# A four-layer kernel for one core: small powers on GpSimd, scan kernels in four column strips, filler products ahead of the first input, and side work in shorter portions

## What is computed

```python
# layer 0 (cut): x is normed, multiplied by w_in, keys and values are compressed
y = _nsa_mixer(_rmsnorm(h, params[0]), *params[1:])
blk = k[:, cmp_idx] + pe[:, None, :]
return jax.nn.silu(blk @ w1) @ w2

# layer 1 (cut): the scan's step and its input factor
dt = jnp.exp(log_dt.astype(f32))[:, None]
mag = jnp.exp(lre * dt)
ab_re = mag * jnp.cos(lim * dt)
ab_im = mag * jnp.sin(lim * dt)
den = lre * lre + lim * lim
coef_re = (nr * lre + ab_im * lim) / den
coef_im = (ab_im * lre - nr * lim) / den
bb_re = coef_re[..., None] * br32 - coef_im[..., None] * bi32
```

## Time and profile before

| | us |
|---|---|
| median of 3 runs | 1860.41 |
| lowest, highest | 1859.4, 1860.86 |
| the profiled execution | 1856.59 |
| its span, first to last instruction | 1854.7 |
| TensorE busy in the span | 1784.1 (96%) |
| VectorE busy | 975.3 (53%) |
| ScalarE busy | 864.8 (47%) |
| GpSimd busy | 164.9 (9%) |
| chain that ended last: TensorE, VectorE, ScalarE | 82%, 10%, 5% |

### The profile page before, as it was taken

The page is one execution under the profiler, slowest core; times in us unless marked ns, Lnnn a source line. Parts: engine busy times, 40 slices in busy tenths (PEclk is TensorE's granted clock), DMA queues, the critical chain, the costliest instruction groups (busy, mean ns, idle before and its releaser), DMA issues.

```text
span 1854.7 us, 24520 instructions
## 1 busy us (share of the span) xinstructions
PE 1784.1 (96%) x9954; PEld 1455.8 (78%) x9954; DVE 975.3 (53%) x1680; ACT 864.8 (47%) x1486; POOL 164.9 (9%) x293
## 2 busy tenths in 40 slices
PE   5899998899999999999999999999999999999997
PEld 4677886679988877876877777888788878888886
DVE  7878556954764365345345545355544544434223
ACT  6355666645454244246345554266633643223223
POOL 2000226510000000000000000022200011111000
PEclk9899999999999999999999999999999999999999
DMA  3563441035423323311322223222132223322332
GB/s 132 159 213 122 132 115 58 1 100 212 151 95 102 103 80 115 101 57 48 111 90 80 69 70 101 94 69 63 55 108 94 92 69 100 102 94 88 105 94 65
DMA packets 61471, 181.30 MB, mean 98 GB/s; under 512 B 7136, under 2 KB 20256, under 8 KB 58928
## 3 DMA queue, kind: packets, MB, share of 16 engines
q1 hardware_dynamic: 61360, 179.75, 29.9%
HBM read 165.57 MB, written 16.25 MB: 98 GB/s over the span
## 4 chain that ended last, share of the span: by engine, by line
PE 82%; DVE 10%; ACT 5%; issue 1%; POOL 1%; DMA 0%; SPq 0%; DVEq 0%; ACTq 0%
PE bank L1002 19%; PE bank L1004 19%; PE bank L1003 18%; PE bank L1096 2%; PE bank L1097 2%; PE bank L1098 2%; PE bank L1259 2%; DVE wlo L2116 1%; PE bank L1238 1%; ACT L1525 1%; PE bank L1022 1%; PE bank L1023 1%; PE bank L1024 1%; PE bank L1228 1%; PE bank L1118 1%
## 5 line engine op out<-in xcount | busy, mean ns | idle before, releaser
L2116 DVE TENSOR_TENSOR wlo<-wraw,whi 128x1024 fp32r<-128x1024 f32 (+1 forms) x262 | 316.4, 1210 | 276.4 <-ACT whi L1520 275.2
L1002 PE MATMUL bank<-Hh,whi 128*128 128x512 f32 (+2 forms) x1104 | 442.9, 401 | 12.2 <-DVE wlo L2116 12.2
L1004 PE MATMUL bank<-Hh,wlo 128*128 128x512 f32 (+2 forms) x1104 | 432.4, 392 | 0.0
L1003 PE MATMUL bank<-Hl,whi 128*128 128x512 f32 (+2 forms) x1104 | 432.1, 391 | 0.0
L1520 ACT ACTIVATE whi<-wraw 128x1024 fp32r<-128x1024 f32 (+1 forms) x262 | 271.9, 1041 | 297.5 <-PE bank L1004 227.6
L1002 PEld LDWEIGHTS bank<-Hh,whi 128*128 128x128 f32 (+2 forms) x1104 | 206.9, 187 | 69.2 <-DVE wlo L2116 14.1
L1004 PEld LDWEIGHTS bank<-Hh,wlo 128*128 128x128 f32 (+2 forms) x1104 | 207.0, 188 | 45.9
L1003 PEld LDWEIGHTS bank<-Hl,whi 128*128 128x128 f32 (+2 forms) x1104 | 207.1, 188 | 44.8 <-issue 1.7
L1525 ACT ACT_TABLE_LOAD x102 | 130.9, 1283 | 2.9 <-DVE epst L2141 1.1
L2889 POOL TENSOR_SCALAR bs<-dist 128x256 f32<-128x256 f32 x16 | 7.4, 460 | 796.7 <-DMA dist<-in_c_dist 795.9
L1002 PE MATMUL bank<-Bh,whi 128*128 128x512 f32 x192 | 75.8, 395 | 0.0
(11 more groups left out here) (393 smaller groups left out, 3230.7 us busy)
## 6 DMA issues: line engine op xcount, KB each, us to landing
wraw<-in_w_o SPq DMA_DIRECT2D x24, 512.0 KB, 3.5
wraw<-in_w_bgate SPq DMA_DIRECT2D x24, 512.0 KB, 3.5
wraw<-in_w_branch SPq DMA_DIRECT2D x24, 512.0 KB, 3.4
wraw<-in_w_fg SPq DMA_DIRECT2D x22, 512.0 KB, 3.5
wraw<-in_w_fu SPq DMA_DIRECT2D x22, 512.0 KB, 3.5
wraw<-in_w_glu SPq DMA_DIRECT2D x16, 512.0 KB, 3.5
wraw<-in_w_fd SPq DMA_DIRECT2D x16, 512.0 KB, 3.5
scratch_CA<-CA SPq DMA_DIRECT2D x4, 1152.0 KB, 6.6
```

The costliest lines, as they stand in the source:

```text
L1002: pe.matmul(o, wh[:, cols], hi(k), start=k == 0, stop=False)
L1003: pe.matmul(o, wh[:, cols], lo(k), start=False, stop=False)
L1004: m = pe.matmul(o, wl[:, cols], hi(k), start=False, stop=k == K - 1)
L2116: dve.tensor_tensor(c.wlo[q][:, 0:n], c.raw[i % RR][:, 0:n], c.whi[q][:, 0:n].bitcast(F32), S_).then_inc(*up(DID, ("wlo", i)))
```

## The change

1. `prep` 2 to 7 are taken out of the side work and stand behind `sines`; their ops run on GpSimd (`cmul` there), `pr` behind `pw`. VectorE keeps `prep` 0, 1 and 8.
2. TensorE multiplies ones by ones, 128x128 in f32, 18 times before and 26 times after the sum of squares (`warm`), into banks that are overwritten later.
3. The kernels' 16 products of a block go to four column strips in turn; Kp, its skip input and its store (8 DMAs for 4) follow that shape.
4. The ticks in w_kvc 2 and 3, w_gate and w_ksw are 3, 2 and 2 for 4, and 4 for 3 in the first two pieces of w_vsw.

```diff
     def pair(self, keys, src):
         for key in keys:
             self.tiles[key] = (src, KT, 128)
-            self.bank.take(key)
+            if key not in self.bank.of:
+                self.bank.take(key)
...
         self.step("nsa_in")
-        self.inv("x", 0, 7, 0, 1.0 / D, "rs")
+        self.bank.take(("total", "x"))
+        self.step("warm", ("total", "x"), 18)
+        self.step("total", "x", 0, 7)
+        self.bank.take(("w_kvc", 0))
+        self.step("warm", ("w_kvc", 0), 26)
+        self.step("inv", "x", 0, 1.0 / D, "rs")
+        self.bank.give(("total", "x"))
         self.tick()
...
         self.step("sines")
+        for part in range(2, 8):
+            self.step("prep", part)
...
         for n in range(2, 4):
-            self.filled("w_kvc", n, 4)
-        self.filled("w_gate", 0, 4, M=48)
+            self.filled("w_kvc", n, 3)
+        self.filled("w_gate", 0, 2, M=48)
         for t in range(4):
-            self.filled("w_ksw", t, 4)
+            self.filled("w_ksw", t, 2)
...
             if j < 2:
-                self.tick(3)
+                self.tick(4)
...
     def prep(self):
-        for part in range(9):
+        for part in (0, 1, 8):
             self.step("prep", part)
             yield
...
+    def warm(key, n):
+
+        on.wait_ge(*before(plan.bank, key))
+        on.wait_ge(*at("ones"))
+        on.wait_ge(*at("x", 0))
+        for _ in range(n):
+            pe.matmul(bank(key)[:, 0:128], c.ones[:, :], c.ones[:, :], start=True, stop=True)
...
-        for q in range(4):
+        for q in range(2):
             for i in range(2):
-                for hf in range(2):
-                    p = 4 * hf + q
-                    x = pe.matmul(k[hf * 32:hf * 32 + 32, q * 128:q * 128 + 128], c.Bd[:, i, p, :],
+                for g in range(4):
+                    p = 2 * g + q
+                    x = pe.matmul(k[g * 32:g * 32 + 32, q * 128:q * 128 + 128], c.Bd[:, i, p, :],
...
         else:
-            tt(s(11), s(1), s(1), M)
...
+        elif part == 8:
+            on.wait_ge(*at("power1"))
+            tt(s(5), s(1), s(1), M)
...
         if n == 0 and i == 0:
             on.wait_ge(*at("Cq", b))
+            on.wait_ge(*at("pw"))
...
+        if part == 2:
+            gp.memset(P(0, 0), 1.0).then_inc(*up(DID))
+            gp.memset(P(1, 0), 0.0).then_inc(*up(DID))
+            on.wait_ge(*at("mag"))
+            on.wait_ge(*at("sin"))
+            rot(P(0, 1), s(4), s(9), M)
+            rot(P(1, 1), s(4), s(10), M, ("power1",))
+            cmul(P(0, 2), P(1, 2), P(0, 1), P(1, 1), P(0, 1), P(1, 1), t1, t2)
...
-        for hf in range(2):
+        for g in range(4):
             for h in range(2):
-                dst = c.dK[b][:, 8 * hf:8 * hf + 8, :].rearrange("c (q h) n -> c q h n", h=2)[:, :, h, :]
-                src = c.Kp[hf * 32 + h * 16:hf * 32 + h * 16 + 16, :, :, :].rearrange("p q k n -> p q (k n)")
+                dst = c.dK[b][:, 4 * g:4 * g + 4, :].rearrange("c (q h) n -> c q h n", h=2)[:, :, h, :]
+                src = c.Kp[g * 32 + h * 16:g * 32 + h * 16 + 16, :, :, :].rearrange("p q k n -> p q (k n)")
```

More of the change, by code:

```diff
@@ L1493, in wd @@
         x.then_inc(*up(PE, ("wd", u), ("wd", u + 1)))
-    walk(plan, dict(mm=mm, pair=pair, mm_half=mm_half, total_half=total_half, lead=lead, sum_h3=sum_h3, tok=tok, tok_twin=tok_twin, rsS=rsS, rows=rows, total=total, hold=hold, fence=fence, cmp_end=cmp_end,
+    walk(plan, dict(warm=warm, mm=mm, pair=pair, mm_half=mm_half, total_half=total_half, lead=lead, sum_h3=sum_h3, tok=tok, tok_twin=tok_twin, rsS=rsS, rows=rows, total=total, hold=hold, fence=fence, cmp_end=cmp_end,
                     vecs=vecs, gate_t=gate_t, cmp_w1=cmp_w1, cmp_out=cmp_out,
@@ L2296, in prep @@
         lre, lim = c.par[:, 0, :], c.par[:, 1, :]
-        t1, t2 = s(11), s(12)
         if part == 0:
@@ L2315, in prep @@
             ts(s(8), s(8), -1.0, M, float(np.float32(np.pi / 2)), A_, ("angle",))
[L2316 to L2334, removed]
-            tt(s(11), s(1), s(1), M)
-            tt(s(12), lim, lim, M)
-            tt(s(11), s(11), s(12), A_)
-            on.wait_ge(*now(DID))
[L2339 to L2348, removed]
+        elif part == 8:
+            on.wait_ge(*at("power1"))
+            tt(s(5), s(1), s(1), M)
+            tt(s(6), lim, lim, M)
+            tt(s(5), s(5), s(6), A_)
+            on.wait_ge(*now(DID))
+            dve.reciprocal(s(5), s(5)).then_inc(*up(DID))
+            ts(s(6), P(0, 1), -1.0, A_)
+            tt(s(7), s(6), s(1), M)
+            tt(s(8), P(1, 1), lim, M)
+            tt(s(7), s(7), s(8), A_)
+            tt(s(2), s(7), s(5), M)
+            tt(s(7), P(1, 1), s(1), M)
+            tt(s(8), s(6), lim, M)
+            tt(s(7), s(7), s(8), S_)
+            tt(s(3), s(7), s(5), M)
     def prep_b(b):
@@ L2826, in nsa_in, with cmul @@
         gp.memset(c.Kp[:, :, 0:8, :], 0.0).then_inc(*up(DID, ("Kp0",)))
-    def prep(part):
[L2829 to L2833, removed]
+    def cmul(ore, oim, xr, xi, yr, yi, t1, t2, *names):
+        rot(t1, xr, yr, M)
+        rot(t2, xi, yi, M)
+        rot(ore, t1, t2, ALU.subtract)
+        rot(t1, xr, yi, M)
+        rot(t2, xi, yr, M)
+        rot(oim, t1, t2, ALU.add, *names)
+    def prep(part):
+        s = lambda i: c.sm[:, i, :]
+        P = lambda i, k: c.pw[:, i, k, :]
+        t1, t2 = s(11), s(12)
+        if part == 2:
[6 more added lines that the diff above has]
+            cmul(P(0, 2), P(1, 2), P(0, 1), P(1, 1), P(0, 1), P(1, 1), t1, t2)
+        elif part in (3, 4):
+            n = 2 * (part - 2)
+            same = lambda ap: ap.broadcast_to([128, n, 32])
+            cmul(c.pw[:, 0, n + 1:2 * n + 1, :], c.pw[:, 1, n + 1:2 * n + 1, :], c.pw[:, 0, 1:n + 1, :], c.pw[:, 1, 1:n + 1, :],
+                 same(c.pw[:, 0, n:n + 1, :]), same(c.pw[:, 1, n:n + 1, :]), c.sm[:, 11:11 + n, :], c.sm[:, 15:15 + n, :],
+                 *([("pw",)] if part == 4 else []))
+        elif part in (5, 6, 7):
+            if part == 5:
+                on.wait_ge(*now(DID))
+                for k in range(8):
+                    x = gp.tensor_copy(c.pr[:, :, k, :], c.pw[:, :, 7 - k, :])
+                x.then_inc(*up(DID, ("pr",)))
+            src, dst = [((s(9), s(10)), (s(13), s(14))), ((s(13), s(14)), (s(15), s(16))),
+                        ((s(15), s(16)), (c.e8[:, 0, :], c.e8[:, 1, :]))][part - 5]
+            cmul(*dst, *src, *src, t1, t2, *([("e8",)] if part == 7 else []))
     def prep_r(m):
@@ L2978, in store_k @@
         on.wait_ge(*at("Kd", b))
-        for hf in range(2):
+        for g in range(4):
             for h in range(2):
-                dst = c.dK[b][:, 8 * hf:8 * hf + 8, :].rearrange("c (q h) n -> c q h n", h=2)[:, :, h, :]
-                src = c.Kp[hf * 32 + h * 16:hf * 32 + h * 16 + 16, :, :, :].rearrange("p q k n -> p q (k n)")
-                sp.dma_start(dst, src).then_inc(*land(f"st_K{b}", *([("K", b)] if hf and h else [])))
+                dst = c.dK[b][:, 4 * g:4 * g + 4, :].rearrange("c (q h) n -> c q h n", h=2)[:, :, h, :]
+                src = c.Kp[g * 32 + h * 16:g * 32 + h * 16 + 16, :, :, :].rearrange("p q k n -> p q (k n)")
+                sp.dma_start(dst, src).then_inc(*land(f"st_K{b}", *([("K", b)] if (g, h) == (3, 1) else [])))
     def store_w(b, i):
@@ L3163, in first_mixer @@
         self.WT = [self.lent.take(f"WT{i}", [128, 8, 8, 16]) for i in range(2)]
-        self.Kp = self.lent.take("Kp", [64, 4, 16, 16])
-        self.skip = self.lent.take("skip", [64, 4, 4, 16])
+        self.Kp = self.lent.take("Kp", [128, 2, 16, 16])
+        self.lent.at += 2048
+        self.skip = self.lent.take("skip", [128, 4, 2, 16])
     def second_mixer(self, r):
```

16 lines of the change are left out of this document (8 added, 8 removed).

## The result

The changed kernel takes **1865.01 us** in the median of 17 runs (1862.24 to 1868.35), the kernel before 1860.67 in as many; the ratio is 1.0021, 95% interval 1.0015 to 1.0028. It is slower by about 4 us, where I forecast 1859.3 and a range up to 1864.0. The profiled execution took 1867.29 us, span 1865.4 us; VectorE is busy 968.7 us for 975.3, GpSimd 189.3 for 164.9, TensorE 1798.2 for 1784.1.

A forecast was written before the change was run, and what follows sets the result against it. TensorE, carrying 82% of the chain of waits, was taken as the bound. A gain of 4.1 us up to w_q less 3.0 given back made 1.1 us faster than the profiled 1856.6, so 1859.3 in the median's terms; range 1854.5 to 1864.

The forecast's parts named there:

- The fillers: First 50 us: they hide in TensorE's idle time; the pair of tiles runs at the high clock, ending 2.8 us earlier.
- Bd ahead of the evictions, w_gate at 47.4: ScalarE does Bd's four copies before w_kvc's sixteen evictions, so w_gate starts at 47.4, not 45.49; TensorE idles 3.9 us.
- GpSimd's powers at 42.4: Small powers on GpSimd done at 39.9, plus 2.5 us for contention; CA ends at 46.6, before w_gate's split.
- GpSimd late: Rival, 5%: GpSimd's code fetch is not hidden, powers come 6 us later, w_gate starts at 53.2; 1865.1 us.
- Four strips at 1.0: A block's 16 kernel products on TensorE take 1.0 us for 1.94, bounds 0.95 and 1.94.
- w_q at 110.1: TensorE starts w_q near 110.1, 4.1 us earlier than before.
- I take 3.0 back: In w_q and w_vsw, six left-over side steps (8.9 us of VectorE) cost 3.0 us, bounds 0 and 3.6.
- The store of K is 8 DMAs now ... nothing waits: On SP's queue K's store takes 3.5 us for 1.72; weights behind it load three pieces ahead, so nothing waits.
- backlog becomes the bound: Rival, 10%: late side ops stall TensorE in w_vsw's last three weight splits; 8.1 us lost, 4.0 slower, 1864.4 us.
- more than 89.7 us from w_q to the scores: Deciding sign of the 10% backlog rival: time from w_q's first product to attention's first scores exceeds 85.6+4.1 = 89.7 us.

The follow-up runs named there:

- experiment 2: The changed kernel with the scan's kernels in two strips again, four DMAs a store: 1865.35 us, ratio to the kernel before 1.0016.
- Experiment 1: The changed kernel with the last block's first WT stored ahead of its K store and Kp copy: 1861.28 us, ratio to the kernel before 0.9999.
- experiment 3: The changed kernel with the side work's portions as before (4, 4, 4 and 3): 1853.97 us, ratio to the kernel before 0.9960.

## Why the prediction was wrong

- **The fillers**: right. The sum started at 11.74, the pair at 19.77 at the high clock from its first product, and ended near 31 (30.8 forecast). They alone are worth nothing that can be measured.
- **Bd ahead of the evictions, w_gate at 47.4**: right, 47.30. The gap was 4.17 us for 3.9. The stretch at the low clock was longer than I took: 12 products in 5.1 us against 2.7 at full pace, 2.4 us for the 1.5 that I read off 3 us of it. So w_ksw at 55.42 for 54.4. Its length is not fixed: behind a gap of 4.19 us in experiment 2 it was 6 products in 2.6 us.
- **GpSimd's powers at 42.4**: they were there at 39.99; one product of 128x32 took about 0.3 us, but the first five ops, beside two splits, 3.4 us in all. VectorE's first CA waited 0.48 us. This lay within its bounds and cost nothing. The rival "GpSimd late" falls, too: the first rotation began at 29.82, 0.1 us behind the sine, after 14.5 us in which GpSimd had no other work.
- **Four strips at 1.0**: 1.08. Right.
- **w_q at 110.1**: 110.96; the 0.9 is about what the low clock in w_gate cost more. Gain up to here 3.3 for 4.1.
- **"I take 3.0 back"**: the step that failed. I took 3.6 as the most that the left-over steps could cost, by putting VectorE's last add at 88.3 us behind w_q and TensorE's last transposes at 89.2. The add ended at 89.4, and attention's scores started at 90.9, 5.3 past the 85.6 of before instead of 3.6: two gaps of TensorE of 0.43 and 0.76 us and one of 2.11 with slow products behind it. Of the 5.3, 3.1 are waits (3.3 for 0.2) and 2.5 slower products (304 in 71.0 us for 68.5); two more turns of WT (+1.8) and the cheaper kernels (-1.7) cancelled, as forecast. I had a bound for VectorE's last step alone; that TensorE would stall on the way there and run slower behind the stall stood only in the rival. And the sum ended at TensorE's scores and left out what else waits for the last step.
- **"The store of K is 8 DMAs now ... nothing waits"**: the other step that failed, and the larger. I looked behind these DMAs for loads only. The Ws store is behind them, too; through it ScalarE's copies, w_vsw's evictions and GpSimd's bias waited, 4.0 us more between the scores and P. Experiment 1 takes just this away and gives 4.1 us at P, 3.7 in time.
- Sum: 3.3 ahead, 5.3 and 4.0 back, 1.3 of them made up later: 4.7 slower in the profile at 440 us, 4.3 in the medians.
- **The rival "backlog becomes the bound"** had the right sign, the right stage and nearly the time (1864.4), with a chance of 10%; its sign, more than 89.7 us from w_q to the scores, came true (90.9). Its place was half right: the low halves of w_vsw, but more the store, which it did not have; so the nearness of its time is in part luck. I held it down because VectorE had 16 us of idle time in that stage. Those waits (8.7 us for ScalarE) stayed at 9.3 as I had argued, and that argument was one for the rival.

The error behind both steps is the same: I priced the short portions where they take work away, and in the stage that receives it only on the engine that does it. That they gain nothing in front was to be read from the rows: TensorE's gaps in w_ksw come from the chain of evictions, and a VectorE with more time does not shorten it. The same holds of TensorE's part of the side work: in front it falls into gaps, behind w_q each set of kernels and each turn of WT costs its full time (experiment 3).

## What to carry to other kernels

Side work belongs where its engine waits anyway, and is to be moved out of a stage only if that engine's queue sets a wait there; here it was moved from a stage where VectorE and TensorE had waits to spare (VectorE 10.5 us before, 23.8 after) to one that TensorE fills without a gap and that ends in a chain of steps. For the last piece of side work follow every user of its buffers over all queues: a store waits in its issuing queue for whatever stands ahead of it, even if its own data is long there. And look on each in-order engine for a copy that waits for a fresh result ahead of evictions that have nothing to do with it: moving four such copies a block seven steps later was worth 7 us in the changed kernel (1857.81 for 1865.01); with the old portions it was 3 us, which the intervals of the two ratios do not tell from nothing.

## What the runs showed of the hardware

- Small operations of GpSimd and VectorE took longer where they ran beside each other; no run sets apart why. VectorE's two products of 128x128 took 0.76 and 1.05 us in the changed kernel beside GpSimd's powers, and 0.62 later, without them; its sum 0.49 and 0.29. Fourteen GpSimd ops of 128x32 took 12.65 us beside VectorE's CA and WT ops, 0.9 each, where the ones at 33.3 to 33.9 took 0.29 each. Here nothing waited for either.
- The same work in the same place can run at either level of the clock from one execution to the next (0.56 and 0.50 against 1.00 in the stretches above), 1 to 3 us each. The program further on is the same, but these are executions of two kernels. A profile can stand 4 us off its kernel's median, as that of before did, with no difference of the program.
- Sixteen products of 32 output rows took 1.94 us in two strips and 1.08 in four at the high clock, so the strips ran side by side (in four at a granted clock of 0.50 it was 1.94, in the kernel with the strips alone). The Trainium skill (TensorEngine Tiling (Array Packing), Theoretical Speedup) gives up to fourfold for outputs of 32 rows; against 0.24 us a product, an estimate of 3.9 for 16, the rows agree (3.6).
